# Smaller first transfers in another order, a last block of columns closed in two halves, and row products by high weights first, in a two-layer hybrid decoder kernel

## What is computed

```python
for i in range(DEPTH):                      # 2 layers
    m = dsa_stick_mixer(h, ...) if i % 2 == 0 else moba_mixer(h, ...)
    h = layer_norm(DEEPNORM_ALPHA * h + m, ln_mix_g[i], ln_mix_b[i])
    f = swiglu(h, ffn_gate[i], ffn_up[i], ffn_down[i])      # (silu(h@gate) * (h@up)) @ down
    h = layer_norm(DEEPNORM_ALPHA * h + f, ln_ffn_g[i], ln_ffn_b[i])
```

## Time and profile before

| | |
|---|---|
| runs | 612.08, 612.25, 612.9 us (median 612.25) |
| the profiled execution's own time | 612.23 us |
| its span, first to last instruction | 610.5 us, so 1.7 us lie outside |
| VectorE busy | 412.8 us (68%) |
| ScalarE busy | 339.8 us (56%) |
| chain that ended last | PE 97%, DVE 1%, DMA 1% |
| DMA | 109.47 MB, mean 179 GB/s |

### The profile page before, as it was taken

One profiled execution on the slowest core, in us unless ns is written; L12 is line 12 of the kernel. 1 busy time (PEld: TensorE's weight loads), 2 busy tenths in 40 slices (PEclk: granted clock), 3 DMA queues, 4 the chain that ended last, 5 costly groups with the idle time before them and its releaser, 6 DMA issues.

```text
span 610.5 us, 10014 instructions
## 1 busy us (share of the span) xinstructions
PE 601.0 (98%) x3585; PEld 519.3 (85%) x3585; DVE 412.8 (68%) x668; ACT 339.8 (56%) x631; POOL 28.3 (5%) x49
## 2 busy tenths in 40 slices
PE   8999999999999999999999999999999999999995
PEld 7989887888888888888889898878888888888884
DVE  5598656878666566565887677658776656666546
ACT  6686775466555545545556666554564554455530
POOL 1011002110000000000020000002000000000000
PEclk9999999999999999999999999999999999999998
DMA  8757426557656555654447533462875565555401
GB/s 310 238 179 270 138 70 213 168 184 234 229 182 199 179 186 191 204 187 159 145 140 268 173 125 129 143 214 68 262 253 178 185 206 201 178 188 190 138 1 69
DMA packets 30114, 109.47 MB, mean 179 GB/s; under 512 B 3376, under 2 KB 3376, under 8 KB 29952
## 3 DMA queue, kind: packets, MB, share of 16 engines
q1 hardware_dynamic: 28512, 102.77, 50.5%
q0 software_dynamic: 1568, 6.23, 3.0%
HBM read 107.94 MB, written 1.05 MB: 179 GB/s over the span
## 4 chain that ended last, share of the span: by engine, by line
PE 97%; DVE 1%; DMA 1%; issue 0%; DVEq 0%; ACT 0%; SPq 0%
PE bank L1011 27%; PE bank L926 24%; PE bank L989 14%; PE bank L929 12%; PE bank L919 5%; PE bank L968 2%; PE bank L969 2%; PE bank L973 2%; PE bank L1060 2%; PE bank L1071 2%; PE bank L1051 1%; PE bank L1262 1%; PE bank L1104 1%; DMA v<-xT_in 1%; PE bank L1167 1%; PE bank L1074 1%
## 5 line engine op out<-in xcount | busy, mean ns | idle before, releaser
L628 DVE TENSOR_TENSOR wlo<-raw,whi 128x1024 fp32r<-128x1024 f32 x190 | 226.4, 1221 | 65.3 <-ACT whi L337 65.0
L337 ACT CAST whi<-raw 128x1024 fp32r<-128x1024 f32 x190 | 192.6, 1049 | 15.4 <-DMA raw<-stream_in 14.7
L926 PE MATMUL bank<-hTs,whi 128*128 128x512 f32 x640 | 159.9, 392 | 0.0
L926 PEld LDWEIGHTS bank<-hTs,whi 128*128 128x128 f32 x640 | 116.2, 189 | 21.6
L1011 PE MATMUL bank<-whi,oThi 128*128 128x512 f32 x240 | 94.9, 395 | 0.0
L1011 PE MATMUL bank<-whi,oTlo 128*128 128x512 f32 x240 | 93.7, 390 | 0.0
L1011 PE MATMUL bank<-wlo,oThi 128*128 128x512 f32 x240 | 93.5, 390 | 0.0
L929 PEld LDWEIGHTS bank<-hTs,wlo 128*128 128x128 f32 x640 | 87.3, 190 | 6.2
L929 PE MATMUL bank<-hTs,wlo 128*128 128x256 f32 x640 | 89.2, 282 | 0.0
L989 PE MATMUL bank<-hTs,whi 128*128 128x256 f32 x320 | 60.6, 289 | 0.0
L542 ACT COPY kT<-bank 128x256 f32<-128x256 f32 x40 | 14.9, 372 | 70.4 <-PE bank L929 70.4
(11 more groups left out here) (150 smaller groups left out, 672.8 us busy)
## 6 DMA issues: line engine op xcount, KB each, us to landing
raw<-stream_in SPq DMA_DIRECT2D x190, 512.0 KB, 4.6
qT<-ln_rows_in POOLq DMA_DIRECT2D x8, 512.0 KB, 5.0
kT<-stream_in SPq DMA_DIRECT2D x2, 512.0 KB, 5.5
v<-xT_in SPq DMA_DIRECT2D x2, 512.0 KB, 5.5
h<-x_in POOLq DMA_DIRECT2D x1, 1024.0 KB, 9.8
out<-h SPq DMA_DIRECT2D x4, 256.0 KB, 2.1
dist<-consts_in POOLq DMA_DIRECT2D x1, 384.0 KB, 3.8
ukv<-w_uk_in POOLq DMA_DIRECT2D x1, 256.0 KB, 6.9
```

The costliest lines, as they stand in the source:

```text
L337: nc.scalar.copy(whi[:, c % RING, j * HW:(j + 1) * HW], raw[:, c % RAW, j * HW:(j + 1) * HW]).then_inc(whi_ready, 1)
L628: nc.vector.tensor_tensor(wlo[:, c % RING, cols], raw[:, c % RAW, cols], whi[:, c % RING, cols].bitcast(F32), ALU.subtract).then_inc(wlo_r ...
L926: mm(dst[:], whi[:, slot, off + k * P:off + (k + 1) * P], hTs[:, k].rearrange("p j s -> p (j s)"), start=(k == 0), stop=False)
```

## The change

Three independent parts. **Start:** chunk 0 lands as 1024, 512 and 512 columns and xT as blocks 0-1, 2-3 and 4-7; the order on SP is first 0, xT 0, xT 1, first 1, xT 2, first 2. So there are six transfers (512, 256, 256, 256, 512 and 256 KB) instead of four. ScalarE's order is quarter 0, pairs 0 and 1, quarters 2 and 1, pairs 2 and 3, quarter 3, and VectorE's is the same. TensorE has 10 products of zeros and then takes blocks 0 to 3 of tile 0 and of tile 1 first, then blocks 4 to 7 of both. Before chunk 1's first tile it waits for the high weights, and for the low ones only at the third pass. **Rows:** for t=1 `rows_wide` takes the 8 high-weight products first and then the 8 low-weight ones. **End:** the 18 products of 512 columns become 18 of columns 512-767 into bank 7 and 18 of columns 768-1023 into bank 2. VectorE adds bank 7 (512 columns, of which the upper 256 hold the earlier chunks) after the first 18, takes statistics of 256 columns, and after the last product adds bank 2 to the upper 256 columns and takes their statistics. The aggregate reads three groups of statistics instead of two.

```diff
-        FIRST = [slice(i * CW // 2, (i + 1) * CW // 2) for i in range(2)]
+        FIRST = [slice(0, 2 * CW // 4), slice(2 * CW // 4, 3 * CW // 4), slice(3 * CW // 4, CW)]
+        XT = (slice(0, 2), slice(2, 4), slice(4, 8))
...
-        WARM = 11
+        WARM = 10
+        FIRST_AT = (1, 3, 2, 4)
...
-            sp.dma_start(first[:, FIRST[0]], stream[0][:, FIRST[0]]).then_inc(first_loaded[0], 16)
-            for j in range(2):
-                sp.dma_start(hT[:, 4 * j:4 * j + 4], xT[:, 4 * j:4 * j + 4]).then_inc(xT_loaded[j], 16)
-            sp.dma_start(first[:, FIRST[1]], stream[0][:, FIRST[1]]).then_inc(first_loaded[1], 16)
+            first_part(0)
+            xT_part(0)
+            xT_part(1)
+            first_part(1)
+            xT_part(2)
+            first_part(2)
...
             first_quarter(0)
-            first_quarter(1)
             for b in range(4):
-                act.wait_ge(xT_loaded[b // 2], 16)
+                act.wait_ge(xT_loaded[min(b, 2)], 16)
                 nc.scalar.copy(hThi[:, 2 * b:2 * b + 2], hT[:, 2 * b:2 * b + 2]).then_inc(hThi_ready, 1)
-            first_quarter(2)
+                if b == 1:
+                    first_quarter(2)
+                    first_quarter(1)
             first_quarter(3)
...
+                        if t and a and last:
+                            dve.wait_ge(acc_done, 3 * n + 4)
...
+                        if t and a and last:
+                            nc.vector.bn_stats(stats[:, t, 6:12], hh[:, 0:S]).then_inc(stat_done, 1)
+                            dve.wait_ge(chunk_used, NORM_CHUNK[n] + 1)
+                            nc.vector.tensor_tensor(hh[:, S:2 * S], hh[:, S:2 * S], bank[2][:, 0:S], ALU.add
+                                                    ).then_inc(res_done, 1)
+                            dve.wait_ge(res_done, 2 * k + 3)
+                            nc.vector.bn_stats(stats[:, t, 12:18], hh[:, S:2 * S]).then_inc(stat_done, 1)
...
-                for k in range(KT):
-                    cols = slice(k * S, (k + 1) * S)
-                    if k % 2 == 0:
-                        pe.wait_ge(hi_ready, base + k // 2 + 1)
-                    mm(dst, hThi[:, k, toks], whi[:, slots, cols], start=(k == 0), stop=False)
-                    mm(dst, hThi[:, k, toks], wlo[:, slots, cols], start=False, stop=False)
+                for w in (whi, wlo):
+                    for k in range(KT):
+                        if k % 2 == 0 and w is whi:
+                            pe.wait_ge(hi_ready, base + k // 2 + 1)
+                        mm(dst, hThi[:, k, toks], w[:, slots, k * S:(k + 1) * S], start=(k == 0 and w is whi),
+                           stop=False)
+                        if t == 0:
+                            mm(dst, hThi[:, k, toks], wlo[:, slots, k * S:(k + 1) * S], start=False, stop=False)
+                    if t == 0:
+                        break
...
+            def out_half(c, kts, half, first, end):
+
+                dst = (bank[7], bank[2])[half][:, 0:S]
+                for j in range(2):
+                    for q, (w, o) in enumerate(AT_PASSES):
+                        at = j * D + 512 + half * S
+                        last = mm(dst, o[:, kts[j], P:S], w[:, c % RING, at:at + S],
+                                  start=(half == 1 and first and q == 0 and j == 0), stop=(end and q == 2 and j == 1),
+                                  skip_group_check=True)
+                return last
...
+            for half in range(2):
+                ks = range(half * KT // 2, (half + 1) * KT // 2)
+                pe.wait_ge(first_hi, FIRST_AT[half])
+                pe.wait_ge(first_lo, FIRST_AT[half])
+                for part in (ks[0:2], ks[2:4]):
+                    first_products(0, part, whi, hThi)
+                    first_products(0, part, wlo, hThi)
+                first_products(0, ks, whi, hTlo)
+                pe.wait_ge(first_hi, FIRST_AT[2 + half])
+                first_products(1, ks, whi, hThi)
+                first_products(1, ks, whi, hTlo)
+                pe.wait_ge(first_lo, FIRST_AT[2 + half])
+                last = first_products(1, ks, wlo, hThi)
             last.then_inc(chunk_used, 1)
-            pe.wait_ge(wlo_ready, 1)
-            cols_out(bank[5][:, 0:S], 1, 0)
+            pe.wait_ge(whi_ready, 1)
+            for j, (w, a) in enumerate(HT_PASSES):
+                if j == 2:
+                    pe.wait_ge(wlo_ready, 1)
+                for k in range(KT):
+                    mm(bank[5][:, 0:S], w[:, 1, k * P:(k + 1) * P], a[:, k, :], start=(k == 0 and j == 0),
+                       stop=(k == KT - 1 and j == 2))
```

More of the change, by code:

```diff
@@ L123, in build @@
         rinv = small[:, 16:24].rearrange("p (b t) -> p b t", b=4)
-        stats = small[:, 128:152].rearrange("p (t c) -> p t c", t=2)
+        stats = small[:, 104:140].rearrange("p (t c) -> p t c", t=2)
         mv = small[:, 152:156].rearrange("p (t c) -> p t c", t=2)
@@ L132, in build @@
         raw_loaded = [[sem(f"raw_loaded{i}{j}") for j in range(2)] for i in range(RAW)]
-        xT_loaded = [sem(f"xT_loaded{i}") for i in range(2)]
-        first_loaded = [sem(f"first_loaded{i}") for i in range(2)]
+        xT_loaded = [sem(f"xT_loaded{i}") for i in range(3)]
+        first_loaded = [sem(f"first_loaded{i}") for i in range(3)]
         first_hi, first_lo = sem("first_hi"), sem("first_lo")
@@ L239, in _, with first_part, xT_part @@
             half = (slice(0, HW), slice(HW, CW))
-            sp.dma_start(first[:, FIRST[0]], stream[0][:, FIRST[0]]).then_inc(first_loaded[0], 16)
-            for j in range(2):
-                sp.dma_start(hT[:, 4 * j:4 * j + 4], xT[:, 4 * j:4 * j + 4]).then_inc(xT_loaded[j], 16)
-            sp.dma_start(first[:, FIRST[1]], stream[0][:, FIRST[1]]).then_inc(first_loaded[1], 16)
+            def first_part(i):
+                sp.dma_start(first[:, FIRST[i]], stream[0][:, FIRST[i]]).then_inc(first_loaded[i], 16)
+            def xT_part(i):
+                sp.dma_start(hT[:, XT[i]], xT[:, XT[i]]).then_inc(xT_loaded[i], 16)
+            first_part(0)
[4 more added lines that the diff above has]
+            first_part(2)
             for c in range(1, L0_FFN):
@@ L404, in first_quarter @@
             def first_quarter(i):
-                act.wait_ge(first_loaded[i // 2], 16)
+                act.wait_ge(first_loaded[max(i - 1, 0)], 16)
                 nc.scalar.copy(whi[:, 0, QUARTER[i]], first[:, QUARTER[i]]).then_inc(first_hi, 1)
             first_quarter(0)
-            first_quarter(1)
             for b in range(4):
-                act.wait_ge(xT_loaded[b // 2], 16)
+                act.wait_ge(xT_loaded[min(b, 2)], 16)
                 nc.scalar.copy(hThi[:, 2 * b:2 * b + 2], hT[:, 2 * b:2 * b + 2]).then_inc(hThi_ready, 1)
-            first_quarter(2)
+                if b == 1:
+                    first_quarter(2)
+                    first_quarter(1)
             first_quarter(3)
@@ L679, in norm @@
                         hh = h[:, t, a * 512:(a + 1) * 512]
-                        if t and a:
+                        if t and a and last:
+                            dve.wait_ge(acc_done, 3 * n + 4)
+                        elif t and a:
                             dve.wait_ge(chunk_used, NORM_CHUNK[n] + 1)
@@ L686, in norm @@
                         dve.wait_ge(res_done, 2 * k + a + 1)
-                        nc.vector.bn_stats(stats[:, t, 6 * a:6 * a + 6], hh).then_inc(stat_done, 1)
+                        if t and a and last:
[5 more added lines that the diff above has]
+                            nc.vector.bn_stats(stats[:, t, 12:18], hh[:, S:2 * S]).then_inc(stat_done, 1)
+                        else:
+                            nc.vector.bn_stats(stats[:, t, 6 * a:6 * a + 6], hh).then_inc(stat_done, 1)
                         if n == 1 and t == 1 and a == 0:
                             split_lo_half(NORM_CHUNK[n] + AHEAD - 1, 0)
-                    dve.wait_ge(stat_done, 2 * k + 2)
-                    nc.vector.bn_aggr(mv[:, t], stats[:, t]).then_inc(mv_ready, 1)
+                    parts = 3 if last and t else 2
+                    dve.wait_ge(stat_done, 2 * k + parts)
+                    nc.vector.bn_aggr(mv[:, t], stats[:, t, 0:6 * parts]).then_inc(mv_ready, 1)
                     dve.wait_ge(mv_ready, k + 1)
@@ L720, in first_quarter @@
             def first_quarter(i):
-                dve.wait_ge(first_hi, i + 1)
+                dve.wait_ge(first_hi, FIRST_AT[i])
                 nc.vector.tensor_tensor(wlo[:, 0, QUARTER[i]], first[:, QUARTER[i]],
@@ L729, in _ @@
                                         hThi[:, 2 * b:2 * b + 2].bitcast(F32), ALU.subtract).then_inc(hTlo_ready, 1)
-                if b == 0:
+                if b == 1:
+                    first_quarter(2)
                     first_quarter(1)
-            first_quarter(2)
             first_quarter(3)
@@ L1036, in last_out @@
                 for a in range(2):
```

(23 more changed lines are left out.)

## The result

The changed kernel takes 614.77 us, the median of 7 runs from 613.04 to 615.9. Before it was 612.25 us, also the median of 7 runs (612.08 to 612.9). The ratio is 1.0035 with a 95% interval from 1.002 to 1.0049: slower by about 2.5 us, where 1.0 us less was forecast. Its runs are spread over 2.9 us, those of before over 0.8. The profiled execution took 615.57 us with a span of 613.8, which is 3.3 us more than before's span of 610.5.

The account below looks back on a forecast made before the run. TensorE was taken to bound the kernel, busy 601.0 of 610.5 us. Start -0.71, rows 0 and end -0.30 summed to -1.01 us against 612.23, giving 611.2 us, with a range from 610.3 to 612.4.

Parts of the forecast that it names:

- What bounds the kernel: Whole kernel: TensorE busy 601.0 of 610.5 us, idle only at the start, two short early stalls and the tail.
- Part 3, the end, -0.30: Closing products: halves add 0.24 us, shorter VectorE work behind the last product saves 0.54; ends 0 and -0.4.
- Part 2, the rows, 0: Rows products for t=1: no instruction added or removed, no stall, no gain; ends -0.3 and +0.1 us.
- Part 1, the start, -0.71: Kernel start: smaller first parts let chunk 1 start at 12.76 instead of 13.47 us; ends -0.4 and -0.94.
- I take 0.09 us extra for each of the four small parts: Start's landings: a 256 KB part takes 0.71 us, as output stores do, where 422 GB/s would give 0.62.
- the 1.4 us that the text names as a sign of being wrong: Start's transfers: landings over 1.4 us apart for 512 KB would show the forecast wrong.
- The rest of part 1: Start after landings: first real product at 6.2 us, chunk 1 at 12.76, no later operand too late.
- The bound of -0.94: Start: largest gain before TensorE waits for chunk 2's second half, whose remainder was put up to 18.29 us.
- The clock: Start: a rise to 2.4 GHz only at 9 us doubles earlier products' cost, losing up to 0.4 us.
- the rival: Start's gain lost on the way, through late operands at 20 to 60 us or the clock: 611.9 us, chance 0.17.
- The rival "transfers pay a fixed price": Start's transfers: 1.4 us fixed each, paid in turn, two more delay everything behind by 2.8 us: 613.4 us, chance 0.05.
- The chances: Forecast 0.49, front reaching its bound (610.6 us) 0.27, others 0.17 and 0.05; faster 0.42, within 0.2% 0.53, slower 0.05.

Follow-up runs that it names:

- the two fast layouts: Changed kernel with its six first parts read from arrays laid end to end, 610.97 us, or with rows padded to 10 KB apart, 610.85 us.
- The five kernels with slow first transfers: Changed kernel 614.77; only chunk 0 end to end 614.08; before with six transfers 617.1, parts cut at partition 64 615.36, xT in 2 KB runs 616.18 us.

## Why the prediction was wrong, point by point

- **What bounds the kernel:** right. The whole difference lies where TensorE was said to be idle, in the start and the tail; the 3.56 us lost at the start stand in the span, less the end.
- **Part 3, the end, -0.30:** right, -0.27. The 36 products took 4.32 us as worked out, the add 0.42 and the statistics 0.43. Of the two prices for a product, the row was right: 0.12 us for 256 columns. The formula that the Trainium skill, page "TensorE: Matmul & The Clock Gate", section "Back-to-back issue gap", gives for an isolated product makes 0.109 us and would have made -0.5 of this part; the measurement decides.
- **Part 2, the rows, 0:** right; the excess of the first product stayed. That the wait before it is its cause was not tested.
- **Part 1, the start, -0.71:** wrong by more than 4 us in the profiled execution, and this is the step that failed: "I take 0.09 us extra for each of the four small parts". It was priced by the output's 256 KB stores, whose pieces are 2 KB too. But those pieces lie 4 KB apart and are written, and the new parts lie 8 KB apart and are read. The row matched in size and not in address or direction. From 4 to 8 us the changed kernel moved 241 and 186 GB/s where 369 was assumed, and xT's second part landed at 8.88 us, 2.7 us after the 6.2 in which 0.18 was allowed for two small parts. The rows of before held a warning. Of the four landings only the last two are 1.25 us apart; between xT's two parts lie 2.02 us (6.05 and 8.07 in the earlier trace rows), over the 1.4 us that the text names as a sign of being wrong.
- **The rest of part 1 held once the parts landed in time,** and was too cautious. In the two fast layouts TensorE's first product came at 5.96 and 6.05 (6.2 forecast), chunk 1 at 12.45 and 12.00 us (12.76 forecast), and the time at 610.97 and 610.85 (611.2 forecast). TensorE met no wait beyond the start in either. The bound of -0.94 was passed because chunk 2's last remainder was ready at 17.66 and 17.50 us, earlier than before's 17.93; the text had it up to 18.29.
- **The clock** was named as a way to lose "up to 0.4 us". It cost about 1.2 us in the medians (614.77 against 613.56 with twenty zeros). The sum of the rival assumed a rise at 9 us; it came at about 14, and some 22 of the 44 products behind the wait ran at the lower level, none of which hid behind a wait.
- **The rival "transfers pay a fixed price",** chance 0.05, gave 613.4 us. Its time was the nearest, and the delay it named for what follows, 2.8 us, is what chunk 1's landing shows (13.31 - 10.58 = 2.73). Its mechanism was wrong: four transfers of 2 KB runs are as slow, and seven transfers end to end are not slow at all. By the Trainium skill, "DMA: Bandwidth & Descriptors", section "Bandwidth", transfers should be batched to 1 MiB. This change came out slower, as that rule would have it, but the runs don't bear the rule out as the reason: six parts of the same sizes gave a loss of 2.5 us or a gain of 1.3 by the distance of their rows. The price of a small read had no row that matched it, and the range, which ended at 612.4, held nothing for that.
- **The chances** don't quite follow from their own rule: a third of 0.49 and all of 0.27 make 0.43 for faster, and half of 0.05 makes 0.03 for slower, where the text has 0.42 and 0.05.
- **The shares of the 2.5 us,** by the medians: the rows and the end -0.2; the start's small parts and new order, when the parts land in time, -1.0 to -1.2; the 8 KB distance +3.8 to +3.9, of which about 1.2 is the clock's.

## What to carry to other kernels

When a transfer is cut along its rows, the pieces become shorter but their distance in memory stays; price it with a row that has the same piece, distance and direction, and if there is none, treat the cost as open. A padded row or an array per part is a change of the host's layout alone, and turned a loss of 2.5 us into a gain of 1.3 here. A test that cuts a transfer another way should keep all 128 partitions in each, or it measures something else. Where TensorE waits soon after its warm-up products, look at the distance between the products behind the wait, and count the lower clock as well as the wait; the clock column showed 1.00 here while they were 0.213 us apart.

## What was not expected of the hardware

- Where all small parts were 2 KB pieces 8 KB apart, 163 to 258 GB/s were moved between 4 and 8 us (three kernels); with the same pieces 10 KB apart it was 368 to 383, and with them end to end 286 and 385. From 8 to 14 us the changed kernel moved 382 to 418 GB/s, though chunk 0's second part, of such pieces, landed only at 10.06 us, so the slowness belongs to the first microseconds as well. Why it ends there stays open.
- Transfers that reach 64 of the 128 partitions with 4 KB rows went at 231 to 238 GB/s between 4 and 12 us, against 358 to 422 for 128 partitions.
- The five kernels with slow first transfers and ten or eleven zeros took from 614.08 to 617.1 us, and the spread of the changed kernel's runs, 2.9 us, fell to 1.0 (10 runs, 610.78 to 611.77) when only its sources were laid end to end.
